# First stage of a two-block transformer kernel: inputs loaded first, modulation parts in four column groups, first projection's products run part by part

## The reference, cut to what matters

```python
sh1x, sc1x, g1x, sh2x, sc2x, g2x = split((silu(c) @ w_ada + b_ada)[:, None, :], 6)
sh1c, sc1c, ...                  = split(silu(c_ctx) @ w_ada + b_ada, 6)
hc = rms_norm(ctx, norm1_g) * (1 + sc1c) + sh1c      # 256 x 1024
hx = rms_norm(x,   norm1_g) * (1 + sc1x) + sh1x      # 256 x 1024
k, v, lr = split(hc @ w_in[:, OFF_KVG:])             # k is the first projection computed
z = hx @ w_in                                        # u, vs, q, r, ga, gb, k, v, lr
...                                                  # gated linear attention, gating, FFNs, second block
```

## Time and profile before

| | |
|---|---|
| time, three runs | 1298.95, 1297.55, 1298.3 us (median 1298.3) |
| the profiled execution | 1298.18 us; its span 1296.4 us; 1.8 us lie around the span |
| busy share of the span | TensorE 97%, weight loads 90%, VectorE 57%, ScalarE 55%, GpSimd 68% |
| mean granted TensorE clock | 0.983 of 2.4 GHz |
| bytes moved | 217.7 MB, mean 168 GB/s |

### The profile page before, as it was taken

The page is one execution under the profiler, slowest core; times in us unless marked ns, Lnnn a source line. Parts: engine busy times, 40 slices in busy tenths (PEclk is TensorE's granted clock), DMA queues, the critical chain, the costliest instruction groups (busy, mean ns, idle before and its releaser), DMA issues.

```text
span 1296.4 us, 26257 instructions
## 1 busy us (share of the span) xinstructions
PE 1258.9 (97%) x9123; PEld 1165.9 (90%) x9123; DVE 740.1 (57%) x1663; ACT 708.0 (55%) x1278; POOL 878.7 (68%) x386
## 2 busy tenths in 40 slices
PE   9999999999999999999789999999999999999997
PEld 3688899999988898898589989999999999999986
DVE  3989851232487773468675346555633776555632
ACT  3656554554666664476333247666655556666653
POOL 0447956588869879754333218888798787888795
PEclk9999999999999999989889899999999999999999
DMA  9985265446546656633222215555566555655562
GB/s 372 403 324 192 82 212 162 127 155 189 179 144 200 191 170 189 199 99 98 81 66 66 66 32 154 188 176 181 156 179 187 179 179 157 192 183 183 154 192 77
DMA packets 66020, 217.71 MB, mean 168 GB/s; under 512 B 9896, under 2 KB 17320, under 8 KB 62608
## 3 DMA queue, kind: packets, MB, share of 16 engines
q1 hardware_dynamic: 65936, 216.56, 51.6%
HBM read 215.48 MB, written 1.05 MB: 167 GB/s over the span
## 4 chain that ended last, share of the span: by engine, by line
issue 40%; POOL 36%; PE 21%; ACT 1%; POOLq 1%; DVE 1%; ACTq 0%; DVEq 0%
POOL w_lo L642 35%; PE bank L750 9%; PE bank L1083 5%; PE bank L842 3%; PE bank L851 1%; PE bank L846 1%; POOL w_lo L649 1%; POOLq L639 0%; ACT h L1597 0%; POOLq L641 0%; ACT w_hi L1597 0%; PE bank L688 0%; PE bank L896 0%; PE bank L693 0%; PE bank L689 0%
## 5 line engine op out<-in xcount | busy, mean ns | idle before, releaser
L642 POOL TENSOR_TENSOR w_lo<-w_raw,w_hi 128x1024 fp32r<-128x1024 f32 x340 | 814.5, 2407 | 379.9 <-ACT w_hi L1597 379.1
L1597 ACT ACTIVATE w_hi<-w_raw 128x1024 fp32r<-128x1024 f32 (+1 forms) x372 | 378.0, 1020 | 124.7 <-PE bank L851 41.2
L750 PE MATMUL bank<-a_hi,w_hi 128*128 128x264 f32 (+3 forms) x704 | 200.7, 285 | 0.1
L750 PE MATMUL bank<-a_hi,w_lo 128*128 128x264 f32 (+3 forms) x704 | 200.4, 285 | 0.0
L750 PE MATMUL bank<-a_lo,w_hi 128*128 128x264 f32 (+3 forms) x704 | 200.2, 284 | 0.0
L727 PE MATMUL bank<-a_parts,w_hi 128*128 128x256 f32 x960 | 173.8, 284 | 0.2
L727 PEld LDWEIGHTS bank<-a_parts,w_hi 128*128 128x128 f32 x960 | 149.8, 192 | 1.1 <-ACTq L1854 0.5
L727 PE MATMUL bank<-a_parts,w_lo 128*128 128x256 f32 x480 | 136.0, 283 | 0.0
L750 PEld LDWEIGHTS bank<-a_hi,w_hi 128*128 128x128 f32 x704 | 133.0, 189 | 0.4 <-DVE a_lo L3487 0.3
L750 PEld LDWEIGHTS bank<-a_lo,w_hi 128*128 128x128 f32 x704 | 133.0, 189 | 0.1
L750 PEld LDWEIGHTS bank<-a_hi,w_lo 128*128 128x128 f32 x704 | 133.0, 189 | 0.0
(11 more groups left out here) (520 smaller groups left out, 2811.6 us busy)
## 6 DMA issues: line engine op xcount, KB each, us to landing
w_raw<-in_s SPq DMA_DIRECT2D x284, 512.0 KB, 3.6
w_raw<-in_down SPq DMA_DIRECT2D x48, 512.0 KB, 3.5
adaw<-in_w_ada SPq DMA_DIRECT2D x16, 1024.0 KB, 9.8
w_raw<-in_down SPq DMA_DIRECT2D x24, 384.0 KB, 3.1
adab<-in_w_ada_first SPq DMA_DIRECT2D x8, 1024.0 KB, 8.7
ctxt<-in_ctx SPq DMA_DIRECT2D x1, 1024.0 KB, 11.4
x<-in_x SPq DMA_DIRECT2D x1, 1024.0 KB, 15.3
out_h<-h SPq DMA_DIRECT2D x4, 256.0 KB, 2.6
```

The costliest lines, as they stand in the source:

```text
L642: pool.tensor_tensor(w_lo[:, s], w_raw[:, s], w_hi[:, s].bitcast(F32), ALU.subtract) \
L750: ins = mm(banks[bank][:, tk], w_[:, s, k], x_[:, k, tk], start=(m == 0), stop=(m == 3 * KD - 1))
L1597: return nc.scalar.activation(out_, in_, f, **kw)
```

## The change

The loads are put in another order: `ctxt`, `x`, `averages`, `pv` directly behind `ident`, then part 0 of `w_ada_first`, units 0 to 3, and parts 1 to 3. `mod_rows` uses a stationary operand of 32 columns (`c2_wide`, two of them filled, the rest zero) and writes tile `k` to the partitions 32 (k mod 4) of the bank: four column groups, two products in each. `modrow` is therefore 128 partitions high, and the flip is four float32 products with `row_pick` (128 x 2, ones at every 32nd row), which add the four groups; they go to the same bank 6 or 7. TensorE computes both sums of squares first, then part 0; then for each `j` all four slots with `k` = 2j and 2j+1, with `mod_rows(j + 1)` after slot 1 and `flip_rows(j + 1)` after slot 3. The waits `mod_taken` on slots 2 and 3 go away (bank 2 and 3 are no longer written by the flip).

```diff
 SyncE
+            small(ctxt[:], a["ctx"], ctx_in)
+            small(x[:], a["x"], x_in)
+            small(averages[:], a["averages"], ctx_in)
+            small(pv[:], a["pv"], ctx_in)
+            ada_blocks(0)
             for s in range(SLOTS):
                 stream_unit("s0", s, s)
+            for j in range(1, 4):
+                ada_blocks(j)          # j >= 2 waits for ada_done j - 1
 GpSimd
+            pool.memset(c2_wide[:], 0.0).then_inc(fills, 1)
 TensorE, mod_rows(j)
+                    pe.wait_ge(mod_taken, j - 1)       # j >= 2
-                    ins = mm(banks[6 + j % 2][0:2, :], c2[:, k], adab[j % 2][:, k], start=(k == 0), stop=(k == KD - 1))
+                    g = 32 * (k % 4)
+                    ins = mm(banks[6 + j % 2][g:g + 32, :], c2_wide[:, k], adab[j % 2][:, k], start=(k < 4), stop=(k >= 4))
 TensorE, flip_rows(j)
-                    ins = nc.tensor.transpose(banks[2 + j % 2][:, 2 * i:2 * i + 2],
-                                              modrow[:, j % 2, i * P:(i + 1) * P], ident[0:2, 0:2])
+                    ins = mm(banks[6 + j % 2][:, 2 * i:2 * i + 2], modrow[:, j % 2, i * P:(i + 1) * P], row_pick[:],
+                             start=True, stop=True)
 TensorE, the order
-            mod_rows(0)
-            mod_rows(1, 5, lambda: mean_square(RMS_CTX))
-            flip_rows(0)
-            mod_rows(2, 1, lambda: mean_square(RMS_X))
-            flip_rows(1)
-            mod_rows(3)
-            flip_rows(2)
-            for s, k0, k1_ in ((0, 0, 4), (1, 0, 4), (0, 4, 6), (1, 4, 6), (2, 0, 6), (3, 0, 6)):
...
+            mean_square(RMS_CTX)
+            mean_square(RMS_X)
+            mod_rows(0)
+            flip_rows(0)
+            for j in range(4):
+                for s in range(SLOTS):
+                    if j == 0:
+                        pe.wait_ge(lo_ready, s + 1)
+                        pe.wait_ge(banks_free, s + 1)
+                    ins = tile_blocks(s, 2 * j, 2 * j + 2)
+                    if j == 3:
+                        ins.then_inc(unit_used, 1)
+                    elif s == 1:
+                        mod_rows(j + 1)
+                if j < 3:
+                    flip_rows(j + 1)
 ScalarE
-            mod_rows(0)
             act.wait_ge(x_in, 16)
...
             root(RMS_CTX, N1, 0)
             root(RMS_X, N1, 0)
+            mod_rows(0)
+            round_unit(0, 0)
             modulated(0)
             round_unit(1, 1)
             round_unit(2, 2)
             round_unit(3, 3)
+            for j in range(1, 4):
+                mod_rows(j)
+                modulated(j)
 VectorE
+            v.tensor_reduce(row_pick[:], ident[:].rearrange("p (g i) -> p i g", i=32)[:, 0:2], mybir.AxisListType.X, ALU.add)
```

More of the change, by code:

```diff
@@ L135, in bass_two_blocks @@
         c2 = sb("c2", [P, KD, 2])
+        c2_wide = sb("c2_wide", [P, KD, 32])
+        row_pick = sb("row_pick", [P, 2])
         stats = sb("stats", [P, 2, 2, 6])
@@ L162, in bass_two_blocks @@
         adab = [at(f"adab{i}", [P, KD, 4 * P], arena + o_) for i, o_ in enumerate((69632, 36864))]
-        modrow = at("modrow", [2, 2, 4 * P], arena + 4096)
+        modrow = at("modrow", [P, 2, 4 * P], arena + 4096)
         ADA_RING = [5, 6, 0, 1, 2, 3, 4, 5, 6, 0, 1, 4, 0, 1, 4, 1]
@@ L506, in _, with ada_blocks @@
             small(ident[:], a["ident"], first_in)
-            for j in range(4):
+            def ada_blocks(j):
                 if j >= 2:
@@ L513, in _ @@
                     sp.dma_start(adab[j % 2][:, ks_], a["w_ada_first"][j][:, ks_]).then_inc(ada_in[j % 2][half], 16)
[L514 to L520, removed]
+            small(ctxt[:], a["ctx"], ctx_in)
[3 more added lines that the diff above has]
+            ada_blocks(0)
             for s in range(SLOTS):
                 stream_unit("s0", s, s)
+            for j in range(1, 4):
+                ada_blocks(j)
             small(wlr[:], a["w_lr"], small_in)
@@ L984, in _, with mod_rows @@
             pe.wait_ge(csil_ready, 1)
-            def mod_rows(j, behind=None, beside=None):
+            def mod_rows(j):
                 if j >= 2:
                     pe.wait_ge(modrow_ready, j - 1)
+                    pe.wait_ge(mod_taken, j - 1)
                 for k in range(KD):
@@ L1661, in root @@
                 fn(rstd[:, c0:c0 + n], banks[bank][:, c1:c1 + n], ACT.Sqrt, bias=eps6[:, e:e + 1]).then_inc(std_ready, 1)
-            act.wait_ge(fills, 2)
+            act.wait_ge(fills, 3)
             act.wait_ge(first_in, 32)
-            fn(c2[:], c2[:], ACT.Silu).then_inc(csil_ready, 1)
+            fn(c2_wide[:, :, 0:2], c2[:], ACT.Silu).then_inc(csil_ready, 1)
             nc.scalar.preload_act_table(ACT.Sqrt)
@@ L1675, in mod_rows @@
                     act.wait_ge(mod_flipped, j - 1)
-                fn(modrow[:, j % 2], banks[6 + j % 2][0:2, :], ACT.Copy).then_inc(modrow_ready, 1)
+                fn(modrow[:, j % 2], banks[6 + j % 2][:, :], ACT.Copy).then_inc(modrow_ready, 1)
             def modulated(j):
@@ L2536, in _ @@
             dve.wait_ge(first_in, 32)
+            v.tensor_reduce(row_pick[:], ident[:].rearrange("p (g i) -> p i g", i=32)[:, 0:2], mybir.AxisListType.X, ALU.add) \
+                .then_inc(warm, 1)
+            dve.wait_ge(first_in, 32)
             v.tensor_reduce(eye16[:], ident[:].rearrange("p (b i) -> p i b", i=BLOCK), AX.X, ALU.add)
@@ L2558, in _ @@
                 dve.wait_ge(mod_flipped, j + 1)
-                shift_, scale_ = (banks[2 + j % 2][:, 4 * part:4 * part + 4].rearrange("p (k j) -> p k j", j=2) for part in range(2))
+                shift_, scale_ = (banks[6 + j % 2][:, 4 * part:4 * part + 4].rearrange("p (k j) -> p k j", j=2) for part in range(2))
                 v.tensor_tensor(mod[:, :, two].rearrange("p j k -> p k j"), shift_, twice(b_ada[:, 0, two]), ALU.add)
```

12 lines of the change are left out of this document (1 added, 11 removed).

## The result

The changed kernel takes 1319.69 us (median of four runs, 1319.28 to 1322.78), the kernel before 1297.92 in the same session: ratio 1.0162, 95% interval 1.0143 to 1.0180. The change costs 21.8 us. The forecast was 1321, its range 1309 to 1332.

A forecast was written before the change was run, and what follows sets the result against it. TensorE was taken to bound the kernel through the first block. A projection ending 14.0 us later, 4.8 and 1.5 of clock and a 2.3 logit wait make 22.6, on 1298.18: 1320.8, given as 1321, range 1309 to 1332.

The forecast's parts named there:

- TensorE sets the time, and nothing behind the stage has slack: TensorE through the first block: a microsecond saved or lost in the first stage reaches the end.
- Loads at nothing: Reordered loads: all arrive in time, cost nothing, with 6 us of cover; `adaw` loads start about 49.5 us.
- Start: Before part 0: squares from 10.8 us, `mod_rows(0)` from 18.6, VectorE ready for part 0 at about 22.3.
- M: TensorE's time for one part's products in four column groups: 3.8 us, pairs of records overlapping only partly.
- rival A: Products of parts: the four groups run fully at once, M = 1.7; +14.8 us, 1313; chance 0.28.
- The wait behind the flip: Slot 0 behind each flip: TensorE stands still 3.8 us for VectorE's operands, four times.
- The clock: TensorE's lower clock around its waits: 1.5 us at the start and 1.2 in each of four periods.
- Behind the projection: First logit: VectorE's lead shrinks by 6.0 us, past 2.5 of slack, so TensorE waits 2.3 for `lrs`.
- The sum: First stage flip to flip: 13.9 us per period, projection ends at 76.2 us, 14.0 later; total 22.6 slower.
- B: Products of parts: no overlap between column groups, M = 6.9; +33 us, 1331; chance 0.16.
- D: First stage much slower: M = 6.9, flips 2.1 us each, every burst cold; 1340 us; chance 0.06.
- C: Slot 0 behind each flip: operands come early and the saved work arrives, up to 6 us faster, 1292; chance 0.05.

The follow-up runs named there:

- e1: The changed kernel with all eight products of a part in one column group instead of four; 1340.06 us.
- e7: The changed kernel with products of parts and flips as early as data allow, first four `adaw` loads not held, tenth modulation behind `lrs`; 1306.08 us.
- e9: e8 with only the first half of each `adaw` load read, so a part of the modulation is left out; 1293.53 us.
- e3: The changed kernel with the products of later parts and their flips moved ahead, so matmuls lie between flip and products; 1304.83 us.
- e11: e8 with the loads reordered to leave no gap, part 3 three slots later, and two modulations behind the logits as in e10; 1304.19 us.
- e6: e3 with the first four `adaw` loads no longer held by the third part (`ada_done` 3); 1304.14 us.
- e4: The changed kernel with 32 more warm-up matmuls at the start and ten unread matmuls behind every flip; 1310.95 us.
- e5: The changed kernel with VectorE's tenth modulation product behind `lrs` instead of in front of it; 1321.16 us.
- e10: The changed kernel with VectorE's tenth and eleventh modulation products behind all the logits; 1319.93 us.
- e12: e11 with VectorE's modulations again in the order of the changed kernel; 1298.11 us.
- e2: The kernel before with the four column groups and wider flips alone, its loads and order kept; 1299.20 us.
- e8: e7 with 32 more warm-up matmuls at the start and ten unread matmuls behind the first flip; 1301.90 us.

## Why the prediction came out right, and where it did not

*TensorE sets the time, and nothing behind the stage has slack.* Held: of the 22.4 us that e1 adds ahead of `w_q`, 20.4 came through. The other direction did not: e7 to e9 show that time won ahead of `w_v` is lost there, so "a microsecond that the stage saves reaches the end" was wrong beyond about the old state. The prediction didn't need it.

*Loads at nothing.* Held in the changed kernel: no wait for a load in the first 120 us. Its `adaw` loads started at 47.9 us (predicted 49.5), and with the stage 13 us longer they were in time. The cover is the lateness itself: take that away (e3), and TensorE waits 4.3 us at `w_v`. The gap in the loads has a part in it, as e11, which has none, waits 2.7 though it gets there 5.7 us earlier; e6 closes little of the gap and waits 4.2.

*Start.* Predicted: squares 10.8, `mod_rows(0)` 18.6, VectorE ready 22.3. Measured: 11.1, 19.53, `mod` at 23.3. The missing microsecond is the first mean square at half clock: in e4, with the clock up, `mod_rows(0)` starts at 18.59.

*M, the products of a part: the term of the sum that was mis-sized.* Taken 3.8, measured 1.92, near rival A's 1.7. The argument from the pairs failed; e1 shows that the groups alone do it. It made the sum about 7 us too long (1.9 in each of four parts, less a little in part 0, where VectorE would have been ready no sooner than 22.3). The Trainium skill's other rule, that weight loads pass running matmuls only into other row groups ("TensorE: Matmul & The Clock Gate", Part 3), was read as 6.9: here all groups use the same rows and a part took 1.92, so the measurement goes against that reading of it. The earlier trace rows spoke against it beforehand: weight loads are listed for 90% and matmuls for 97% of one span, so they overlap, although most of this kernel's matmuls use all 128 rows.

*Flips.* 0.8 taken, 0.95 to 1.05 measured.

*The wait behind the flip.* Predicted 3.8 us of standing per part, measured 2.67 and 0.80, 3.5, in the later three and 2.8 in part 0; 13.2 us in seven waits. Shown by e3, which moves nothing but the products of parts and the flips and starts `w_q` 12.3 us earlier, waits and their clock losses together.

*The clock.* Predicted 1.5 at the start and 1.2 per period, 6.3; measured 1.3, 1.2 and three times some 1.4, so 6.7. By the Trainium skill's rule that I had set beside the sum, that every short burst between recurring waits runs cold ("TensorE: Matmul & The Clock Gate", Part 1, HAM oscillation), the term would have been 8.3. The trace agrees with it in that the half clock comes back in each of the three later periods (0.50 to 0.52), and disagrees in that only the burst behind the second wait is slow; the one between the waits runs at 1.00. The row that I had called in agreement with the rule is no case of it: it has no waits, TensorE is listed as busy for all 3.70 us ahead of the half clock. What the clock costs net in the stage is 5.3 (e4), as part of it falls where TensorE would otherwise wait.

*Behind the projection.* Predicted a wait of 2.3 us at the first logit, measured 2.65. Not foreseen: 1.5 us of half clock behind it. e5 and e10 show that another order of VectorE's work only moves this wait.

*The sum.* With M = 1.92 and the rest as predicted the stage would have come out about 7 us shorter and the total at about 1313, rival A, whose condition came true and whose time did not. What filled the difference: 0.4 more clock in the stage, 1.5 behind the logit, and 3.6 at 560 us. That last one is not settled. ScalarE's waits for weight loads from 520 to 600 us are 7.5 us in the changed kernel and 4.7 before, the wait of TensorE 2.85 in the changed kernel, 2.1 in e1, 1.5 in e3, 0.3 in e4 and 0.7 before and in e12, but also 1.9 in e2, whose `w_q` starts only 0.6 us later than before; that it follows the loads' phase is argued only, and no run isolates it. So that 1321 lies so near to 1319.7 is luck: one term was too large by about 7, three were too small by 5.5 together, and two of these (behind the logit and at 560 us) stood at nothing in the sum.

*The rivals.* B (no overlap) and D needed M = 6.9: e1 shows how that would look, 1340, where B had said 1331; D had said 1340, but with flips of 2.1 us, which took 1.05. C (faster) needed the operands in time and no clock loss; e3 and e7 gave the first, e8 both, and it still didn't come out faster, because the loads were next (e9).

## What to carry to other kernels

Before you shorten an engine's work, look at what it covers: here 16 us less of products on TensorE gave nothing (e2): their time went into waiting for loads and into half clock. When a small product makes the operand of the next big one, put other work between the two, at least as long as the chain through the other engines (here 4.3 us), or the chain is exposed each time and the clock falls as well. And an engine off the path that is fed late (VectorE here) isn't helped by a new order of its work: the wait came back elsewhere (e5, e10).

## What the runs showed of the hardware

- Float32 products with 32 stationary columns, in four column groups, overlap nearly in full, though each is two records and all use the same rows: 16 records in 1.92 us, 7.05 in one group (e1).
- Idle time of 2.67 and 0.80 us around about 1 us of matmuls was followed each time by a stretch of about 3 us at 1.2 GHz; matmuls that nobody reads, in the same places, kept it at 2.4 GHz. `w_q` started 5.3 us earlier and the kernel was 8.7 us faster (e4).
- The same instructions don't get the same clock in every execution: behind 6.4 to 8.0 us of waiting the first mean square took 2.90 us each time, but the second took 1.53 us in the changed kernel, e1 and e6, and 2.90 in e3, e5, e7 and e10.
